# Compression of the cached rows in a hybrid decoder step: products by row halves of the array, in high and low parts, in place of full-array fp32 products on regrouped rows

## The reference, cut to what matters

```python
def compress(rows, pe, w1, w2):
    B, L = rows.shape[:2]
    n_sub = L // CMP_STRIDE
    ...
    sub = rows[:, :n_sub * CMP_STRIDE].reshape(B, n_sub, CMP_STRIDE, ATT_KV_HEADS, HEAD_DIM)
    u = jnp.einsum('bnsgd,jsdh->bjngh', sub, w1.reshape(n_part, CMP_STRIDE, HEAD_DIM, CMP_HIDDEN))
    pre = jnp.einsum('sd,sdh->h', pe, w1)
    for j in range(n_part):
        pre = pre + u[:, j, j:j + n_blk]
    return jnp.einsum('bngh,hd->bngd', jax.nn.silu(pre), w2)
```

## Time and profile before

| | us |
|---|---|
| median of 3 runs | 1761.43 (1761.41 to 1762.59) |
| the profiled execution's own time | 1759.75 |
| its span | 1757.9 |
| PE busy in the span | 1673.5 (95%) |
| DVE busy | 1147.0 (65%) |
| ACT busy | 781.6 (44%) |
| the compression's fills, first product to last | 631 to 855 of the span |

### The profile page before, as it was taken

The page is one execution under the profiler, slowest core; times in us unless marked ns, Lnnn a source line. Parts: engine busy times, 40 slices in busy tenths (PEclk is TensorE's granted clock), DMA queues, the critical chain, the costliest instruction groups (busy, mean ns, idle before and its releaser), DMA issues. The chain is left out here.

```text
span 1757.9 us, 32955 instructions
## 1 busy us (share of the span) xinstructions
PE 1673.5 (95%) x11975; PEld 1435.2 (82%) x11975; DVE 1147.0 (65%) x2535; ACT 781.6 (44%) x1652; POOL 426.6 (24%) x546
## 2 busy tenths in 40 slices
PE   6999999999998989988878999999999999999999
PEld 5999999788886856555546877999999999977887
DVE  6632248776676745565354368887778788687885
ACT  6322453777775535445334234322322232365342
POOL 1321111776664643343341001000000000040000
PEclk9999999999999999999998999999999999999999
DMA  6623111121001366566674231322222332593343
GB/s 164 106 98 115 47 43 26 28 50 27 18 12 37 88 250 199 168 210 230 210 258 173 73 99 64 115 91 97 90 90 94 107 113 84 175 383 96 93 120 108
DMA packets 158859, 204.25 MB, mean 116 GB/s; under 512 B 55110, under 2 KB 109423, under 8 KB 158674
## 3 DMA queue, kind: packets, MB, share of 16 engines
q1 hardware_dynamic: 136058, 121.66, 23.3%
q0 software_dynamic: 22368, 80.46, 13.2%
q10 hardware_dynamic: 312, 0.52, 0.1%
HBM read 164.69 MB, written 37.90 MB: 115 GB/s over the span
## 5 line engine op out<-in xcount | busy, mean ns | idle before, releaser
L3073 PE MATMUL banks<-u_sum,w_sum 128*128 128x264 f32 x2904 | 358.1, 284 | 2.7 <-DVE w_sum L3104 2.7
L3073 PEld LDWEIGHTS banks<-u_sum,w_sum 128*128 128x128 f32 x2904 | 355.0, 189 | 4.4 <-DVE w_sum L3104 4.3
L494 PE MATMUL banks<-u_parts_mix,w_in_parts 128*128 128x352 f32 x1440 | 248.2, 329 | 3.4 <-DVE u_parts_mix L877 3.4
L494 PEld LDWEIGHTS banks<-u_parts_mix,w_in_parts 128*128 128x128 f32 x1440 | 232.0, 189 | 8.5 <-DVE u_parts_mix L877 3.8
L2177 ACT ACTIVATE turned<-banks 128x512 f32<-128x512 f32 (+1 forms) x136 | 78.7, 587 | 144.7 <-PE banks L2040 116.7
L2052 PE MATMUL banks<-turned,cmp_w 128*128 128x512 f32 x256 | 133.8, 605 | 6.7 <-DVE turned L2179 3.7
L3412 PE MATMUL banks<-wd_hi,gd_hi 128*128 128x512 f32 x308 | 120.2, 390 | 1.4 <-DVE gd_lo L3443 1.0
L3412 PE MATMUL banks<-wd_lo,gd_hi 128*128 128x512 f32 x308 | 120.0, 390 | 0.0
L2040 PEld LDWEIGHTS banks<-consts,rows_grouped 128*128 128x128 f32 x512 | 64.4, 144 | 68.0 <-issue 59.8
L3412 PE MATMUL banks<-wd_hi,gd_lo 128*128 128x512 f32 x308 | 119.9, 389 | 0.0
L3300 POOL DMA_DIRECT2D rest_whole<-g_rest x1 | 0.6, 594 | 466.6 <-issue 466.6
(11 more groups left out here) (474 smaller groups left out, 3440.6 us busy)
## 6 DMA issues: line engine op xcount, KB each, us to landing
gd_whole<-g_sums SPq DMA_DIRECT2D x77, 256.0 KB, 2.7
g_sums<-silu_gate SPq DMA_DIRECT2D x55, 256.0 KB, 2.1
w_gate_raw<-in_w_gate SPq DMA_DIRECT2D x11, 1024.0 KB, 5.5
w_up_raw<-in_w_up SPq DMA_DIRECT2D x11, 1024.0 KB, 5.3
w<-in_w_down POOLq DMA_DIRECT2D x33, 256.0 KB, 19.2
w_in_raw<-in_w_in SPq DMA_DIRECT2D x29, 256.0 KB, 3.4
g_sums<-s SPq DMA_DIRECT2D x22, 256.0 KB, 2.3
x_tile<-in_x_prompt SPq DMA_DIRECT2D x8, 512.0 KB, 4.5
```

The costliest lines, as they stand in the source:

```text
L494: mm = nc.tensor.matmul(bank[:, 0:PIECE], w[:, pb, :], u[:, pa, k, tokens(p)], start=(k == 0 and (pa, pb) == TERMS[0]), stop=(k == KT - 1 ...
L3073: mm = nc.tensor.matmul(bank(tg, i), wp[side, p][:, a, k, :], m.u[tg, i, b][:, k, :], start=(k == 0 and (a, b) == TERMS[0]), stop=(k == kh ...
```

## The change

- No regrouping: DVE's L2294 copies and `rows_grouped` go. The transposes read the gathered chunk. A transposed piece is now one token with 2 groups x 64 features on its partitions; a fill is still two tokens and 512 columns (t, h, 128).
- For each fill ACT writes the high part, rounded to fp32r, into `turned_hi`, and then DVE subtracts it from the same PSUM bank into `turned_lo` (4 slots). PE's wait for a fill is on the second (`split`).
- The weights are split likewise, in 8 pieces of 128x512 between the first fills (`w1_hi` on ACT, `w1_lo` on DVE), the last 4 (values) after a load that SP issues first in this stage. The weights stand twice, once for each half of the partitions.
- A fill's product is 12 fp32r matmuls of 64 rows, 128 columns and 256 moving columns: 2 tokens x 3 products (high-high, high-low, low-high) x 2 groups, each group on its half of the partitions and into its own bank. Even units use banks 0 and 1, odd ones 6 and 7.
- The compressed scores move from bank 6 to bank 2, the sums of the output change banks with hb, and waits follow (`imp_taken`, `taken`, `added`).
- All 128 compression fills are copied by ACT (80 were). The SSD roots come at fill 15, the SSD scaling at odd fills from 17. The window's values are loaded after the last compression fill. A ring slot is freed by the turning of its chunk, not by its regrouping.

```diff
+    for j in range(2):
+        for half in range(2):
+            sp.dma_start(raw[64 * half:64 * half + 64, :, j, :],
+                         io.cmp_w1[0, kv, CSTRIDE * j:CSTRIDE * (j + 1), :, :].rearrange("t d h -> d t h")).then_inc(loaded, 16)
...
         if kind == "comp":
-            return order[f][2] % 2 == 1 or order[f][2] == 4
+            return True
...
+                load_cmp_weights(sp, io, w.raw_v, 1, s.w1_in)
                 sp.wait_ge(s.zeroed, 1)
...
-                load_values(0)
...
+                used(sp, "comp", 15, 7)
+                load_values(0)
...
                         if kind == "comp":
-                            pool.wait_ge(s.grouped, 4 * hb + 2 * h + sh + 1)
+                            pool.wait_ge(s.turned, at["comp", hb, 4 * h + 3] + 1)
...
-                        G = 2 * u + q // 4
-                        pe.wait_ge(s.grouped, 2 * G + 2)
-                        pieces = [(w.xr[:, G % 2, h, g * 512 + (q % 4) * P:g * 512 + (q % 4 + 1) * P], P)
-                                  for g in range(NG) for h in range(2)]
+                        if q % 4 == 0:
+                            for h in range(2):
+                                chunk_here(pe, ("comp", u, q // 4, h))
+                        pieces = [(ring(("comp", u, q // 4, h))[:, (2 * (q % 4) + t) * P:(2 * (q % 4) + t + 1) * P], P)
+                                  for t in range(2) for h in range(2)]
...
+                    if u < 2 and q % 2 == 0:
+                        pe.wait_ge(s.w1_lo, 4 * u + q // 2 + 1)
                     if q == 0:
-                        if u == 11:
+                        if u == 12:
                             pe.wait_ge(s.w_taken, 1)
-                        elif u == 12:
                             pe.wait_ge(s.s_taken, 4)
                         elif u >= 2:
                             pe.wait_ge(s.added, 2 * u - 2)
-                    mm = nc.tensor.matmul(m.bank[u % 2][:, :], m.cmp.w1[:, u % 2, q, :, :].rearrange("p j h -> p (j h)"),
-                                          w.fill[:, f % SLOTS, :], start=(q == 0), stop=(q == 7))
+                    hi, lo = w.fill_hi[:, f % SLOTS, :], w.fill_lo[:, cmp_number[f] % LOWS, :]
+                    for t in range(2):
+                        for i, (weights, x) in enumerate(((w.w1_hi, hi), (w.w1_hi, lo), (w.w1_lo, hi))):
+                            for g in range(NG):
+                                rows = slice(64 * g, 64 * g + 64)
+                                mm = nc.tensor.matmul(cmp_bank(u, g)[:, 0:256], weights(u % 2, 2 * q + t)[rows, :],
+                                                      x[rows, 256 * t:256 * t + 256], start=(q == 0 and t == 0 and i == 0),
+                                                      stop=(q == 7 and t == 1 and i == 2))
...
+                def w1_hi(piece):
+                    if piece == 4:
+                        act.wait_ge(s.w1_in, 16 * 4)
...
-                ssd_roots()
+                w1_hi(0)
...
+                        if f >= 16 and f % 2 == 1 and scales:
                             ssd_scale(*scales.pop(0))
+                    if f % 2 == 0 and f // 2 + 1 < 8:
+                        w1_hi(f // 2 + 1)
+                    if f == 15:
+                        ssd_roots()
...
+                def low_part(f):
+                    n = cmp_number[f]
+                    dve.wait_ge(s.copied_a, copies_before[f])
+                    if n >= LOWS:
+                        used(dve, "comp", (n - LOWS) // 8, (n - LOWS) % 8)
+                    nc.vector.tensor_tensor(w.fill_lo[:, n % LOWS, :], m.bank[3 + f % 3][:, :], w.fill_hi[:, f % SLOTS, :].bitcast(F32),
+                                            ALU.subtract).then_inc(s.split, 1)
```

More of the change, by code:

```diff
@@ L1517, in _ @@
             def _(sp):
[L1518 to L1521, removed]
+                load_cmp_weights(sp, io, w.raw, 0, s.cmp_loaded)
                 for b in range(0, DB, 2):
@@ L1850 @@
 SSD_STORES = 16 * (4 * DB // 2 + 4)
-SLOTS = 8
+SLOTS, LOWS = 8, 4
 HW_ = CSTRIDE * DKV // 2
@@ L1907, in sample_attention @@
     LAST_OF_FOURTH = at["comp", 3, 7]
-    first_of = {at["comp", u, 4 * sh]: 2 * u + sh for u in range(16) for sh in range(2)}
+    cmp_number = {at["comp", u, q]: 8 * u + q for u in range(16) for q in range(8)}
+    cmp_bank = lambda u, g: m.bank[((0, 1), (6, 7))[u % 2][g]]
+    out_bank = lambda hb, other: m.bank[((0, 1), (7, 6))[hb][other]]
     n_fills = len(order)
@@ L1922, in sample_attention @@
     copies_before = [sum(1 for x in ACT_FILLS[:f + 1] if x == ACT_FILLS[f]) for f in range(n_fills)]
-    with stage(nc, "zeroed q_placed turned copied_v copied_a used grouped w2_in win_k_in win_v_in shifted added hidden_done projected "
+    with stage(nc, "zeroed q_placed turned copied_v copied_a split used w1_in w1_hi w1_lo imp_taken w2_in win_k_in win_v_in shifted added hidden_done projected "
                    "taken squared k_sums k_rstd k_normed c_scored c_ready c_exp c_weights imp_done masked "
@@ L1928, in copied @@
         def copied(engine, f):
-            engine.wait_ge(s.copied_a if ACT_FILLS[f] else s.copied_v, copies_before[f])
+            if f in cmp_number:
+                engine.wait_ge(s.split, cmp_number[f] + 1)
+            else:
+                engine.wait_ge(s.copied_a if ACT_FILLS[f] else s.copied_v, copies_before[f])
         def used(engine, *fill):
@@ L2086, in importance @@
                     pe.wait_ge(s.c_weights, hb + 1)
-                    nc.tensor.matmul(m.bank[6][:, 0:255], c("rep_sum"), w.pc[:, 0:255], start=True,
+                    nc.tensor.matmul(m.bank[2][:, 256:511], c("rep_sum"), w.pc[:, 0:255], start=True,
                                      stop=True).then_inc(s.imp_done, 1)
@@ L2124, in weigh @@
                     copied(pe, f)
-                    if hb and i == 0:
-                        pe.wait_ge(s.o_ready, 1)
+                    if i == 0:
+                        pe.wait_ge(s.added, (30, 32)[hb])
                     if i < 8 and i % 2 == 0:
@@ L2226, in compressed_exp @@
                         weights_turned(act, 8)
-                    nc.scalar.activation(w.pc[:, 0:255], m.bank[6][:, 0:255], ACT.Exp, bias=w.nm[:, hb, 0:1],
+                    nc.scalar.activation(w.pc[:, 0:255], m.bank[2][:, 0:255], ACT.Exp, bias=w.nm[:, hb, 0:1],
                                          accum_out=w.sum[:, hb, 0:1]).then_inc(s.c_exp, 1)
@@ L2355, in block_scores @@
                     dve.wait_ge(s.imp_done, hb + 1)
-                    chain(nc.vector.tensor_copy(w.imp[:, 1:256], m.bank[6][:, 0:255]))
+                    nc.vector.tensor_copy(w.imp[:, 1:256], m.bank[2][:, 256:511]).then_inc(s.imp_taken, 1)
+                    dve.wait_ge(s.imp_taken, hb + 1)
                     chain(nc.vector.tensor_reduce(w.score[:, 0:64], w.imp[:, 1:257].rearrange("p (j x) -> p j x", x=4),
```

111 lines of the change are left out of this document (65 added, 46 removed).

## The result

The changed kernel takes **1794.72 us** (median of 4 runs, 1791.47 to 1796.6), the kernel before in the same session 1761.42 (1758.2 to 1762.59): ratio 1.019, 95% interval 1.0169 to 1.0211. It is 33.3 us slower. The prediction said slower, 1783 with a range of 1768 to 1803: the direction and the range held, and the size came out a third too small (21.6 us against 33).

A forecast was written before the change was run, and what follows sets the result against it. PE was taken to bound the kernel; 17 us for 128 fills and once-only terms (-1.5 + 4 - 1.9 + 0.5 + 2 + 1.5) gave +21.6 on 1759.75, so 1781.4, as a median 1783 us, range 1768 to 1803.

The forecast's parts named there:

- the sum over the fills: Compression stage on PE: a fill goes from 1.30 to 1.43 us, 0.13 x 128 = 17 us more.
- The halves run together, the pair costs 0.118: Fill's products on PE: two half-array products overlap at 0.118 us a pair, six pairs 0.71; bounds 0.107 and 0.24.
- Rival 2: Fill's products on PE: half-array products do not overlap, 0.24 us a pair, +110 us, 1875 us; chance 5%.
- Changing the shape costs 0.28 per fill: Between turnings and products on PE: two changes of array shape per fill, 0.14 us each; bounds 0 and 0.35 per fill.
- Rival 1: Between turnings and products on PE: changing to row halves is free, a fill takes 1.15 us, 1747 us; chance 6%.
- The start, -1.5: Start of the compression: no wait for the first regrouping, first product at about 629.6; -1.5 us (0 to -2.5).
- The value weights, +4: Fill 7: the 1 MB load, slowed by gathers, lands by 641.5 and delays PE's product; +4 us (0 to +15).
- the clock, +0.5: Early compression: a wait for the weights brings half clock again, in exchange for that of the start; +0.5 us (-1.7 to +3).
- The two old waits go, -1.9: Early compression: PE's waits of 1.25 and 0.69 us, which came with DVE's queue at a regrouping, disappear; -1.9 us.
- The roots at fill 15, +2: ACT's queue amid the copies: table loads and short operations take 4.4 us, 1.4 of each fill hidden; +2 us (0 to +4.5).
- Units 11 to 13, +1.5: Late compression: ACT has four exponentials, table loads and now all copies; +1.5 us (0 to +5).
- Rival 3: Compression stage: ACT's queue becomes the bound, with value weights at 650 and half clock after; 1795 to 1810 us; chance 13%.

The follow-up runs named there:

- the whole-array run: Against the kernel before: no regrouping, rows and weights split, three fp32r products on the whole array per fill, not computing the reference; 1731.24 us, ratio 0.9965.

## Why the prediction was right or wrong

- **What bounds the kernel, and the sum over the fills:** right. PE paces the stage, and 25 of 33 us are the fills' own time.
- **The halves run together, the pair costs 0.118:** right, 0.12 in the timeline, 0.24 on the same half. Rival 2 (halves take turns) is out.
- **Changing the shape costs 0.28 per fill:** the mechanism was right, the size was not. It is 0.34, inside of the bounds of 0 and 0.35. The reading of the earlier trace rows was right for the earlier trace rows: the starts of single records there give 0.15 in the block of turnings, rounds of 0.109, and 0.03 more for the first round and 0.11 for the last, 0.29 in sum. What failed is to carry it over to another shape. Between the full array and its row halves the block of turnings is stretched by the same 0.15, but the first product by 0.10 in place of 0.03, and the last by 0.09. With that the fill is 1.49 and not 1.43: 25 us in place of 17, the largest part of what was missing. The Trainium skill's rule that a change of tiling mode drains the engine (TensorEngine Tiling, Key Properties) agrees with the 0.34 us per fill, though the trace shows a price and not a drain; its factor of 2 (Theoretical Speedup) with the 0.12 against 0.24 of a pair alone. Rival 1, the free change, is out.
- **The start, -1.5:** right. From the last state-space turning to the first product it was 6.9 us before and is 5.5 after.
- **The value weights, +4, and the clock, +0.5:** too small. PE waited 5.24 us (10.42 on the third chip) near 652, not 4 near 640. The load was issued from 630.1 and not at 627.5, and still nearly all of it was there at the predicted 641.5: on the third chip, whose trace has all 64 landings, 48 at 641.5 and 57 at 642.1. What the prediction lacked is that the split waits for the last of them, which came at 650.66 (651.78 there), 8 us or more behind the bulk. From 642 to 650 the DMA engines moved 370 GB/s and more, the gathers, the window's keys (1 MB) and the state's store among them, which I had not put in that queue; without the gathers the last landing stood at 637.92. The clock's share was mis-sized with it. What is left of the stretch beside the fills (25) and the idle time (6.3 us more) is 3.5 us, and the granted clock is 0.96 in place of 0.98.
- **The two old waits go, -1.9:** wrong. In their place, at 640 to 641.5, PE has waits of 1.09, 0.32 and 0.43 without a releaser in the trace. On the third chip neither the kernel before nor the change has waits of either kind there, so that DVE's regrouping, which the prediction blamed, is not shown to be their cause.
- **The roots at fill 15, +2:** mis-sized, one wait of 0.72 us at 669.28.
- **Units 11 to 13, +1.5, old waits and all:** about nothing in sum. From 820 to 856 the change has waits of 1.98 and 2.01, and the 4.06 of the earlier trace rows is not there; it is not there in the kernel before on the third chip either, so its going is not shown to be the change's doing. In all, idle time grew by 6.3 us against the 5.6 of my four terms, so their sum was nearly right and the shares were not, which is luck.
- **Ahead of the stage:** 2.7 us in this profile, of which the sum had none; the executions differ by as much without the change.
- **Rival 3** (ACT's queue becomes the bound) was half there: one stall of 5 us, no regular wait. In the whole-array run, where the fill is 0.36 us shorter, the chain ACT to DVE does become a second bound (13.0 us of waits).

## What to carry to other kernels

Count the changes of the array's shape, not only the columns: here a pair of half-array products (0.119 us) was as fast as one of the full array with as many columns (0.12), and every alternation between full and half shape cost 0.34 us, more than what the cheaper arithmetic gave (0.86 to 0.71). Where shapes must alternate, put several fills' products together; pairs, in 49 places, took 18 us off the stretch here, which was not enough to pass the kernel before. And an engine that only waits for weights must not have another unit's copies queued behind it.

## What the hardware did that I had not expected

- Products on different halves of the rows seem to overtake each other. Written group by group (three of one half, then three of the other), they still started in pairs, and the fill took 1.50 us. The time says the same: two products in a row on one half are 0.12 apart, and in the written order a fill would need 8 such steps at least, 0.94 us in place of 0.71. The Trainium skill (TensorE: Matmul & The Clock Gate, Step-by-step: what each phase is for) says that only the loading of weights is pulled ahead and the matmuls stay in program order. Between two halves of the array this run shows otherwise, by the starts that the profiler records. It is one run, and no view shows the order of the compiled program, for which I take that of the source.
- The price of a change of shape depends on the shape: 0.34 us to row halves and back (0.20 in, 0.15 out), 0.29 to quarter columns and back in the earlier trace rows (0.12 in, 0.17 out).
- A load can be all but landed and still hold its reader: of 64 landings 57 were there by 642.1, the last at 651.78.
- On the third chip, where the kernel before is 23 us faster (1738.55 against 1761.94), the change is slower by 41 us in place of 33. A ratio measured on one chip is not that of another.
